# One-core decoder step on Trainium2: the compression of a unit runs with the next channel tile's products, and the first loads are cut and ordered anew

## The chip, the core and the metric

The kernel runs on one NeuronCore of a Trainium2 chip. That core has five engines that take their instructions in program order and meet at semaphores: TensorE (PE in the profile; its weight loads stand apart as PEld), VectorE (DVE), ScalarE (ACT), GpSimd (POOL) and SyncE (SP). SP and ACT also issue DMAs; sixteen DMA engines carry them. The metric is the device time of one execution in microseconds (us). It was 1530.45 us, the median of three runs from 1529.3 to 1533.97 us.

## What is computed

One inference step of two layers, all in float32, for a prompt of 512 tokens and 8 samples of 8 tokens (576 tokens in all), width 1024. The first layer is a gated depthwise convolution over 2048 channels; the second is attention with a compressed, a selected and a windowed branch. The change touches two pieces of it that share no data: the input product and convolution of the first layer, and the compression of the 8 samples' cached keys and values, which depends on inputs alone.

```python
def conv_mixer(x, state, w_in, b_in, dw_w, dw_b, ln_g, ln_b, w_out):
    h = x @ w_in + b_in
    a, gl, z = jnp.split(h, 3, axis=-1)
    u = a * jax.nn.sigmoid(gl)
    ...
    y = layer_norm(depthwise_31_taps(up), ln_g, ln_b)
    y = jax.nn.silu(y) * jax.nn.silu(z)
    return y @ w_out, new_state

def compress(kseq, pe, w1, b1, w2):
    ...
    h = jnp.einsum("sd,sdh->h", pe, w1) + b1
    for j in range(r):
        h = h + parts[j][:, j:j + nc]        # parts: 16-token chunks times w1
    return jnp.einsum("bcgh,hd->bcgd", jax.nn.silu(h), w2)
```

## The kernel before

**Tiles and units.** The 2048 channels are 16 tiles of 128. For each channel tile `ct`, PE makes two products of the transposed input `xT` (1024 x 576) with 512 KB of weights each: the gate (`product(2 * ct, GL, ...)`, called GL below) and the value (`product(2 * ct + 1, A, ...)`, called A). A product is 16 matmuls in the program, which the trace counts as 32. ACT takes the sigmoid of GL into the one buffer `sgl`, DVE multiplies (L996 to L1000) and then runs the 31 taps (L1014, some 29 us per tile), and POOL does the sample rows and sums. After all channel tiles come 16 Z products on the same line (L1354), and between the second and third of them four matmuls that sum `y` over the channels (L1450, L1451).

The compression is 16 **units** `u` (8 samples, keys and values). A unit's 2 MB of cache pages come into `xc`. It goes in four steps `k`: ACT copies a quarter into `rl` (`regroup`, L721), PE transposes it (`turn`, L1365), ACT copies the result to `xtr` (`turned_out`, L713), and PE multiplies it with `wc` (`hidden`, L1377). ACT then applies silu (L776), and PE multiplies with the second weight (`latent`, L1401 or L1406). In the kernel before, unit `ct` is worked in the loop turn of channel tile `ct`: GL, the transposes of the conv state (`state_turn`, L1387 to L1392), `turn(ct, 0)`, A, `latent(ct - 1)`, then the other three turns and four hiddens. In loop turn 0 the first `turn` stands behind A.

**Order.** Everything is written out by hand, engine by engine. SP issues, in order: x, the sample rows, the page table; then per channel tile the GL weights (L431), the state rows (L436), the A weights (L431), and 16 page loads of 128 KB for the unit (L444), each behind a register load of the page's number. ACT issues the conv parameters (L690 to L693: 37 rows of 2048 floats, one row to one partition of `aux`), small tensors, `wc` (L697) and the second weights (L700, L701) before its first copy. PE starts with the transposes of x (L384; 8 for each of four 128-token tiles and for the 64 sample tokens), waiting for both x loads together (`s_x`), then transposes `aux` (L1342, 16 of 37 x 128) and two small tensors (L1344); after the copies to `pars` (L705, L980) the first GL product may begin. POOL forms the bias sums `cbs` from `wc` (L600 to L604), and PE adds them up at the end of unit 0 (L1433).

**Buffers.** `wi` has 4 slots of weights, `xc` has 3 units (`XBUF`), the page loads of unit u wait until ACT has regrouped unit u - 3 (`rl_ready`). `bank[MISC]` in PSUM is shared in turn by state, latent and bias results; the order of turns is in `state_group` and `latent_group`.

Of the kernel before, what the change touches and what calls it, by code (L numbers as in the profile page):

```python
# [11 lines left out]
P = 128  # L12
# [30 lines left out]
NPAR = TAPS + 6  # L43
UPS = TS + TAPS - 1
# [40 lines left out]
def build_program(nc, x_prompt, x_sample, state_conv, cache_kv, cache_win, page_table,  # L85
# [4 lines left out]
    with ctx:  # L90
# [63 lines left out]
        aux = at(182, DIN)  # L154
        aux2 = at(190, P)
        cbt = at(140, 16 * P).rearrange("p (n h) -> p n h", n=16)
        cbs = at(192, 2 * P).rearrange("p (s h) -> p s h", s=2)
# [60 lines left out]

        def state_group(ct):

            return 1 if ct == 0 else 2 * ct + 1

        def latent_group(u):

            return 2 * u + 4
# [8 lines left out]
        s_small = sem("s_small")  # L234
        s_x = sem("s_x")
# [45 lines left out]
        ring_in = [sem(f"ring_in{r}") for r in range(8)]  # L281
# [142 lines left out]
        def _(sp):  # L424
            sp.dma_start(xr[:, 0:4, :], x_prompt[0].rearrange("(t p) m -> p t m", p=P)).then_inc(s_x, 16)
# [21 lines left out]

            for ct in range(CT):
                if ct >= 2:
                    sp.wait_ge(gl_ps, ct - 1)  # L450
                load_weights(2 * ct, 1, ct)
                if ct >= 2:
                    sp.wait_ge(misc_ps, state_group(ct - 2))
                load_state(ct)
                if ct >= 2:
                    sp.wait_ge(a_ps, ct - 1)
                load_weights(2 * ct + 1, 0, ct)
                if ct == 0:
                    sp.wait_ge(s_pg, 16)
# [38 lines left out]
            def load_group(n):  # L498
                for k in range(KT):
                    if n < 2:  # L500

                        sp.wait_ge(t4_used, 4 * n + k // 2 + 1)
                    elif k == 0:
                        sp.wait_ge(grp_used, n - 1)
                    sp.dma_start(ring[:, n % 2, k], w_in[k * P:(k + 1) * P, GROUPS[n]:GROUPS[n] + 512]
                                 ).then_inc(ring_in[(n % 2) * 4 + k // 2], 16)
# [182 lines left out]
        def _(act):  # L689
            act.dma_start(aux[0:TAPS, :], conv_dw_w[0]).then_inc(s_small, 16)  # L690
            act.dma_start(aux[TAPS:TAPS + 3, :], conv_b_in[0].rearrange("(a n) -> a n", a=3)).then_inc(s_small, 16)
            for r, v in enumerate((conv_dw_b, conv_ln_g, conv_ln_b)):
                act.dma_start(aux[TAPS + 3 + r:TAPS + 4 + r, :], v).then_inc(s_small, 16)  # L693
            act.dma_start(aux2[0:32, :], cmp_pe[0].rearrange("s (q e) d -> (s q) (e d)", e=2)).then_inc(s_small, 16)
            act.dma_start(aux2[32:34, :], cmp_b1[0]).then_inc(s_small, 16)
            for s in range(2):
                act.dma_start(wc[:, s].rearrange("p j q h -> p (j q) h"),  # L697
                              cmp_w1[0, s].rearrange("(q e) d h -> (e d) q h", e=2)).then_inc(s_wc, 16)
# [6 lines left out]
            act.copy(pars[:, 0:8].rearrange("p c n -> p (c n)"), bank[4][:, 0:8 * NPAR]).then_inc(s_aev, 1)  # L705
# [44 lines left out]

            for ct in range(CT):
# [8 lines left out]
                if ct == 0:  # L760
                    regroup(0, 0)
                turned_out(ct, 0)
                regroup(ct, 1)
                if ct:
                    latent_out(ct - 1)
                for k in range(1, STEPS):
                    turned_out(ct, k)
                    if k + 1 < STEPS:
                        regroup(ct, k + 1)
                if ct == 0:  # L770
                    act.wait_ge(misc_ps, 2)
                    act.activation(cb[:, 0:1], bank[MISC][:, 0:1], ACT.Identity, bias=auxT[:, 32:33])
                    act.activation(cb[:, 1:2], bank[MISC][:, 1:2], ACT.Identity, bias=auxT[:, 33:34]).then_inc(misc_ev, 1)
                    act.wait_ge(misc_ev, 2)
                act.wait_ge(xt_used, STEPS * (ct + 1))
                act.activation(hT[:, ct % 2, 0:4 * NC].rearrange("p (g n) -> p g n", g=4),  # L776
                               bank[HID][:, :].rearrange("p (g n) -> p g n", g=4)[:, :, 0:NC],
                               ACT.Silu, bias=cb[:, ct % 2:ct % 2 + 1]).then_inc(h_silu, 1)
                if ct + 1 < UNIT:
                    regroup(ct + 1, 0)  # L780
            state_rows(CT)
            latent_out(UNIT - 1)
# [10 lines left out]
            for i in range(2):  # L793
                silu_z(i)
# [180 lines left out]
        def _(dve):  # L975
# [4 lines left out]
            ch.mark(dve.tensor_copy(pars[:, 8:16].rearrange("p c n -> p (c n)"), bank[5][:, 0:8 * NPAR]))  # L980
# [55 lines left out]
            dve.wait_ge(s_x, 64)  # L1036
# [298 lines left out]
        def _(pe):  # L1335
            pe.wait_ge(s_const, 3)
            pe.wait_ge(s_x, 32)
            for t in range(TT):
                transpose_tile(pe, x_columns, t, PAIRS, s_xps, s_xev)
            pe.wait_ge(s_small, 112)  # L1340
            for c in range(CT):
                pe.transpose(bank[4 + c // 8][:, (c % 8) * NPAR:(c % 8 + 1) * NPAR], aux[0:NPAR, c * P:(c + 1) * P],  # L1342
                             ident[0:NPAR, 0:NPAR])
# [65 lines left out]

            for ct in range(CT):  # L1410
# [8 lines left out]
                if ct == 0:  # L1419
                    turn(0, 0)  # L1420
                    pe.wait_ge(s_wc, 32)
                    pe.wait_ge(s_w2, 48)
                else:
                    latent(ct - 1)
                for k in range(1, STEPS):
                    turn(ct, k)
                    hidden(ct, k - 1)
                hidden(ct, STEPS - 1)
                if ct == 0:
                    pe.wait_ge(s_cbs, 2)  # L1430
                    pe.wait_ge(misc_ev, 1)
                    for s in range(2):
                        last = pe.matmul(bank[MISC][:, s:s + 1], cbs[:, s], ones[:, 0:1], start=True, stop=True)  # L1433
                    last.then_inc(misc_ps, 1)
            state_turn(CT)
            latent(UNIT - 1)

            for i in range(CT):
# [4 lines left out]
                product(2 * CT + i, Z[i % 2], z_ps)  # L1443
                if i == 1:
# [36 lines left out]
            def kv_tile(w, t):  # L1481
# [36 lines left out]
            def wide(j):  # L1518
# [8 lines left out]
                for h in range(2):  # L1527
                    for k in range(KT):
                        if r == 0 and h == 0:
                            pe.wait_ge(ring_in[(n % 2) * 4 + k // 2], 32 * (n // 2 + 1))  # L1530
# [351 lines left out]
```

## Time and profile before

| | us |
|---|---|
| median of 3 runs | 1530.45 |
| the profiled execution | 1531.58 |
| its span, first to last instruction | 1529.9 |
| PE busy | 1434.4 (94%) |
| DVE busy | 818.3 (53%) |
| ACT busy | 476.0 (31%) |
| POOL busy | 480.1 (31%) |

The span is the stretch between the first and the last profiled instruction; 1.7 us of the execution lie outside it. A share of busy time is a mean over stages with different limits, so the stretch around a change is read by itself: the first 60 us, one loop turn, and the end of the loop near 600 us.

### The profile page before, as it was taken

Reading aid. Unit: us, or ns where it says so; the run is one execution under the profiler, and the core shown is the slowest. Engines: PE = TensorE matmul, PEld = TensorE weight load, DVE = VectorE, ACT = ScalarE, POOL = GpSimd, SP = SyncE. Lnnn points to the kernel's source line nnn. Section 1 sums busy time; section 2 is a strip of 40 time slices with the busy share of each in tenths; the row PEclk is TensorE's granted clock in tenths of the full one; section 3 lists DMA queues with packets and bytes.
Section 4 is the critical chain, followed back from the end, with each engine's and each line's share of the span. In section 5 each row is a group of like instructions: output and inputs, shape, how many; then the busy total and the mean of one; then the engine's idle time right before and its main releaser. Section 6 shows DMA issues by size and latency. Waiting matters only on the chain.

```text
span 1529.9 us, 23043 instructions
## 1 busy us (share of the span) xinstructions
PE 1434.4 (94%) x8098; PEld 910.8 (60%) x8098; DVE 818.3 (53%) x1663; ACT 476.0 (31%) x1063; POOL 480.1 (31%) x449
## 2 busy tenths in 40 slices
PE   2999999999999999999999999999988889988886
PEld 2666666666666666777444444877755554455543
DVE  1578887888888888710112311132367774454443
ACT  1243343334434333222100000111355552064552
POOL 0855556566665555411100000000056562000000
PEclk9999999999999999999999999999999999999998
DMA  6543332333333312533510333114000004537870
GB/s 183 137 122 115 91 106 87 93 104 97 95 98 98 96 32 67 190 110 96 228 68 0 115 114 123 50 58 163 28 1 1 2 1 133 184 111 243 256 236 9
DMA packets 139549, 158.38 MB, mean 104 GB/s; under 512 B 16226, under 2 KB 103525, under 8 KB 139237
## 3 DMA queue, kind: packets, MB, share of 16 engines
q1 hardware_dynamic: 134162, 150.07, 31.5%
q10 hardware_dynamic: 5272, 6.83, 1.5%
q8 instruction: 65, 1.06, 0.3%
q14 instruction: 50, 0.41, 0.1%
HBM read 150.18 MB, written 16.38 MB: 109 GB/s over the span
## 4 chain that ended last, share of the span: by engine, by line
PE 84%; SPq 4%; DVE 3%; POOL 3%; issue 2%; ACTq 2%; DMA 2%; ACT 1%; DVEq 0%
PE bank L1354 25%; PE bank L1377 15%; PE bank L1531 8%; PE bank L1466 7%; PE bank L1493 5%; PE bank L1365 4%; PE bank L1693 4%; POOL arena L679 3%; PE bank L1639 2%; SPq L546 2%; PE bank L1670 2%; SPq L548 2%; PE bank L1654 2%; DMA arena<-in_cache_kv_dram 2%; DVE arena L1154 2%
## 5 line engine op out<-in xcount | busy, mean ns | idle before, releaser
L1014 DVE SCALAR_TENSOR_TENSOR arena<-arena 128x512 f32<-128x512 f32 x464 | 424.3, 988 | 0.0
L1354 PE MATMUL bank<-arena 128*128 128x288 f32 x1536 | 381.0, 408 | 0.9 <-DVE arena L981 0.9
L1354 PEld LDWEIGHTS bank<-arena 128*128 128x128 f32 x1536 | 292.0, 191 | 86.5 <-issue 8.3
L1377 PE MATMUL bank<-arena 128*128 128x508 f32 x512 | 239.8, 615 | 0.0
L1377 PEld LDWEIGHTS bank<-arena 128*128 128x128 f32 x512 | 93.3, 190 | 109.8 <-issue 109.8
L613 POOL TENSOR_TENSOR arena<-arena 128x248 f32<-128x248 f32 x128 | 134.1, 1082 | 1.3
L1531 PE MATMUL bank<-arena 128*128 128x288 f32 x512 | 127.0, 407 | 0.6 <-PE bank L1531 0.6
L398 DVE SCALAR_TENSOR_TENSOR arena<-arena,bank 128x512 f32<-128x512 f32 (+1 forms) x20 | 13.6, 680 | 209.8 <-PE bank L1466 160.8
L679 POOL TENSOR_SCALAR arena<-arena 128x128 f32<-128x128 f32 (+3 forms) x96 | 100.3, 1055 | 71.8 <-DVE arena L1162 71.8
L1531 PEld LDWEIGHTS bank<-arena 128*128 128x128 f32 x512 | 96.2, 190 | 27.3 <-issue 1.5
L1466 PE MATMUL bank<-arena 128*128 128x512 f32 x256 | 110.4, 592 | 0.0
L713 ACT COPY arena<-bank 128x512 f32<-128x512 f32 x128 | 68.7, 589 | 108.7 <-PE bank L1365 91.4
L620 POOL TENSOR_TENSOR arena<-arena 128x1024 f32<-128x1024 f32 (+1 forms) x64 | 97.0, 1516 | 5.0
L1154 DVE CUSTOM_DVE_ANT_0 arena<-bank,arena 128x512 f32<-128x512 f32 (+3 forms) x128 | 57.6, 489 | 53.2 <-PE bank L1639 52.8
L1466 PEld LDWEIGHTS bank<-arena 128*128 128x128 f32 x256 | 48.5, 190 | 59.9 <-issue 59.6
L1493 PE MATMUL bank<-arena 128*128 128x512 f32 x192 | 83.3, 593 | 0.6 <-PE bank L1496 0.6
L625 POOL TENSOR_TENSOR arena<-arena 128x576 f32<-128x576 f32 x16 | 18.4, 1147 | 181.7 <-DVE arena L1016 181.7
L1654 PE MATMUL bank<-arena 128*128 128x128 f32 x320 | 54.9, 291 | 20.3 <-POOL arena L679 19.3
L721 ACT COPY arena<-arena 128x512 f32<-128x512 f32 x128 | 73.2, 627 | 0.2 <-DMA arena<-in_cache_kv_dram 0.2
L1365 PEld LDWEIGHTS bank<-arena 128*128 128x128 f32 x512 | 59.1, 141 | 22.1 <-issue 21.1
L886 ACT ACTIVATE arena<-arena 128x512 f32<-128x512 f32 (+3 forms) x128 | 70.8, 556 | 1.5 <-DVE arena L1154 0.8
L1365 PE MATMUL bank<-arena 128*128 128x128 f32 x512 | 66.6, 273 | 2.4 <-ACT arena L721 2.4
(254 smaller groups left out, 1585.7 us busy)
## 6 DMA issues: line engine op xcount, KB each, us to landing
arena<-in_cache_kv_dram SPq DMA_DIRECT2D x256, 128.0 KB, 3.4
arena<-in_cache_kv_dram SPq DMA_DIRECT2D x128, 256.0 KB, 3.2
arena<-in_conv_w_in_dram SPq DMA_DIRECT2D x48, 512.0 KB, 4.2
arena<-in_nsa_w_in_dram SPq DMA_DIRECT2D x56, 256.0 KB, 4.7
arena<-in_conv_w_out_dram SPq DMA_DIRECT2D x16, 512.0 KB, 4.8
arena<-in_cache_win_dram SPq DMA_DIRECT2D x8, 1024.0 KB, 7.1
out_dram<-in_cache_win_dram SPq DMA_DIRECT2D x1, 8064.0 KB
arena<-in_x_prompt_dram SPq DMA_DIRECT2D x2, 2048.0 KB, 9.4
```

The costliest lines, as they stand in the source:

```text
L613: ch.mark(pool.tensor_tensor(terms[:, :, n, 0:TAPS], ups[c][:, :, n:n + TAPS], pars[:, ct:ct + 1, 0:TAPS].broadcast_to([P, NB, TAPS]), ALU ...
L620: ch.link(pool.tensor_tensor(flat[:, :, 0:half], flat[:, :, 0:half], flat[:, :, half:2 * half], ALU.add))
L679: pool.tensor_scalar(w, w, ust[:, 36 + k:37 + k], None, ALU.mult).then_inc(u_sc, 1)
L1014: ch.mark(dve.scalar_tensor_tensor(part, src, w, part, ALU.mult, ALU.add))
L1154: dve.tensor_tensor_reduce(prob[u % SLOTS][:, e, 0:n], bank[2 * (u % 2) + e][:, 0:n], maskrow[:, 512 - n:512], 1.0, BIG, ALU.add, ALU.min, ...
L1354: last = pe.matmul(bank[pair + h][:, 0:HALF], wi[:, n % WSLOT, k], xT[:, k, h * HALF:(h + 1) * HALF], start=k == 0, stop=k == KT - 1)
L1365: last = pe.transpose(bank[TURN + g // 2][:, col:col + P], rlf[:, g, h], ident)
L1377: last = pe.matmul(out, wc[:, s, j, h * STEPS + k], x4[:, h, :, j:j + NC], start=(k == 0 and h == 0 and j == 0), stop=(k == STEPS - 1 and ...
L1466: last = pe.matmul(bank[pair + nh][:, :], y[:, c, t * P:(t + 1) * P], wo[c][:, nh * 512:(nh + 1) * 512], start=c == 0, stop=c == CT - 1)
L1493: last = pe.matmul(bank[t][:, :], x1T[:, k, t * P:(t + 1) * P], slot, start=k == 0, stop=k == KT - 1)
L1531: last = pe.matmul(bank[pair + h][:, 0:HALF], ring[:, n % 2, k, r * P:(r + 1) * P], x1T[:, k, h * HALF:(h + 1) * HALF], start=k == 0, stop ...
L1654: last = pe.transpose(bank[4 + e][:, k * P:(k + 1) * P], prob[u % SLOTS][:, e, k * P:(k + 1) * P], ident)
```

## The change

Five things are changed.

1. The parameters are loaded as 16 partitions (one for each channel tile) of 31, 3 or 1 pieces of 128 floats, instead of as rows of 2048 floats to 31, 3 or 1 partitions. PE then needs 37 transposes of 16 x 128 in place of 16 of 37 x 128, and the copies to `pars` write with a stride.
2. x is loaded in four DMAs of 512 KB with a semaphore each, and PE waits tile by tile.
3. `wc` is issued by SP instead of ACT, behind the first A weights; the weights and state rows of channel tiles 0 and 1 are issued ahead of the first unit's pages.
4. Unit `u` is worked in loop turn `u + 1`; its first `turn` stands ahead of that loop turn's A product. Unit 15 stands behind the loop, and `latent(15)` behind the first Z product.
5. Later, in the second layer, eight semaphores of the weight ring become four, so the first matmul of a group waits for four pieces instead of two.

```diff
-            sp.dma_start(xr[:, 0:4, :], x_prompt[0].rearrange("(t p) m -> p t m", p=P)).then_inc(s_x, 16)
+            for t in range(4):
+                sp.dma_start(xr[:, t, :], x_prompt[0, t * P:(t + 1) * P, :]).then_inc(x_in[t], 16)
...
+            for ct in range(2):
+                load_weights(2 * ct, 1, ct)
+                load_state(ct)
+                load_weights(2 * ct + 1, 0, ct)
+                if ct == 0:
+                    for s in range(2):
+                        sp.dma_start(wc[:, s].rearrange("p j q h -> p (j q) h"),
+                                     cmp_w1[0, s].rearrange("(q e) d h -> (e d) q h", e=2)).then_inc(s_wc, 16)
+            sp.wait_ge(s_pg, 16)
             for ct in range(CT):
                 if ct >= 2:
                     sp.wait_ge(gl_ps, ct - 1)
-                load_weights(2 * ct, 1, ct)
-                if ct >= 2:
+                    load_weights(2 * ct, 1, ct)
...
                 if ct == 2:
-                    sp.wait_ge(misc_ps, 2)
+                    sp.wait_ge(s_aps, 1)
...
-            act.dma_start(aux[0:TAPS, :], conv_dw_w[0]).then_inc(s_small, 16)
+            act.dma_start(aux[0:CT, 0:TAPS], conv_dw_w[0].rearrange("k (c n) -> c k n", c=CT)).then_inc(s_small, 16)
...
+            def unit(u):
+                turned_out(u, 0)
+                regroup(u, 1)
+                if u:
+                    latent_out(u - 1)
...
                 state_rows(ct)
-                if ct == 0:
+                if ct:
+                    unit(ct - 1)
+                else:
                     regroup(0, 0)
...
             state_rows(CT)
-            latent_out(UNIT - 1)
+            unit(UNIT - 1)
...
             pe.wait_ge(s_const, 3)
-            pe.wait_ge(s_x, 32)
             for t in range(TT):
+                pe.wait_ge(x_in[t] if t < 4 else s_x, 16)
                 transpose_tile(pe, x_columns, t, PAIRS, s_xps, s_xev)
             pe.wait_ge(s_small, 112)
-            for c in range(CT):
-                pe.transpose(bank[4 + c // 8][:, (c % 8) * NPAR:(c % 8 + 1) * NPAR], aux[0:NPAR, c * P:(c + 1) * P],
-                             ident[0:NPAR, 0:NPAR])
+            for k in range(NPAR):
+                half, col = divmod(k, PHALF) if k < 2 * PHALF else (1, PHALF)
+                pe.transpose(bank[4 + half][:, col * CT:(col + 1) * CT], aux[0:CT, k], ident[0:CT, 0:CT])
...
                 product(2 * ct, GL, gl_ps)
                 state_turn(ct)
                 if ct:
-                    turn(ct, 0)
+                    turn(ct - 1, 0)
                     pe.wait_ge(a_free, ct)
                 product(2 * ct + 1, A, a_ps)
...
+                if ct:
+                    unit(ct - 1)
             state_turn(CT)
-            latent(UNIT - 1)
+            turn(UNIT - 1, 0)
+            unit(UNIT - 1)
...
                 product(2 * CT + i, Z[i % 2], z_ps)
+                if i == 0:
+                    latent(UNIT - 1)
...
                     if t == 0:
-                        pe.wait_ge(ring_in[(w % 2) * 4 + k // 2], 32 * (w // 2 + 1))
+                        pe.wait_ge(ring_in[(w % 2) * 2 + k // 4], 64 * (w // 2 + 1))
```

**SP at the start of the program.** Before, the rows up to the first page load (128x8x128 is a tile of weights, 120x2x128 the state rows):

```order
L425 DMA arena<-in_x_prompt_dram 128x4x1024
L426 DMA arena<-in_x_sample_dram 64x1024
L427 DMA pages<-in_page_table_dram 1x128
L431 DMA arena<-in_conv_w_in_dram 128x8x128
L436 DMA arena<-in_state_conv_dram 120x2x128
L431 DMA arena<-in_conv_w_in_dram 128x8x128
L443 TENSOR_LOAD pages
```

And now, where line 441 loads weights, 446 state rows and 464 `wc`:

```order
L435 DMA arena<-in_x_prompt_dram 128x1024 x4
L436 DMA arena<-in_x_sample_dram 64x1024
L437 DMA pages<-in_page_table_dram 1x128
L441 DMA arena<-in_conv_w_in_dram 128x8x128
L446 DMA arena<-in_state_conv_dram 120x2x128
L441 DMA arena<-in_conv_w_in_dram 128x8x128
L464 DMA arena<-in_cmp_w_dram 128x16x128 x2
L441 DMA arena<-in_conv_w_in_dram 128x8x128
L446 DMA arena<-in_state_conv_dram 120x2x128
L441 DMA arena<-in_conv_w_in_dram 128x8x128
L453 TENSOR_LOAD pages
```

Five more DMAs stand ahead of the first page load: the two of `wc`, and those of channel tile 1, which stood behind the first unit's 16 pages.

**PE at the start of the program.** Before, from the transposes of x through GL 0 and A 0 (L1354) into unit 0:

```order
L384 MATMUL bank<-arena 128x128 x32
L384 MATMUL bank<-arena 128x64 x8
L1342 MATMUL bank<-arena 128x37 x16
L1344 MATMUL bank<-arena 128x34
L1354 MATMUL bank<-arena 128x288 x16
L1387 MATMUL bank<-arena 128x120 x2
L1354 MATMUL bank<-arena 128x288 x16
L1365 MATMUL bank<-arena 128x128 x16
L1377 MATMUL bank<-arena 128x4x127 x4
L1365 MATMUL bank<-arena 128x128 x8
```

And now (L1373 is the product, L1384 `turn`, L1406 to L1411 the state):

```order
L393 MATMUL bank<-arena 128x128 x32
L393 MATMUL bank<-arena 128x64 x8
L1362 MATMUL bank<-arena 128x16 x37
L1363 MATMUL bank<-arena 128x34
L1373 MATMUL bank<-arena 128x288 x16
L1406 MATMUL bank<-arena 128x120 x2
L1373 MATMUL bank<-arena 128x288 x32
L1406 MATMUL bank<-arena 128x120 x2
L1410 MATMUL bank<-arena 30x128
L1411 MATMUL bank<-arena 64x128
L1384 MATMUL bank<-arena 128x128 x8
L1373 MATMUL bank<-arena 128x288 x16
```

A 0 and GL 1 now follow each other, and the first `turn` of unit 0 stands between GL 1 and A 1.

**PE at the end of the loop.** Before, from the last hiddens of unit 15 to the first sum over channels:

```order
L1377 MATMUL bank<-arena 128x4x127 x8
L1391 MATMUL bank<-arena 30x128
L1392 MATMUL bank<-arena 64x128
L1401 MATMUL bank<-arena 127x64 x4
L1354 MATMUL bank<-arena 128x288 x32
L1450 MATMUL bank<-arena 128x288
```

And now, from the last state transposes to `latent(15)` (L1425 is `latent(14)`, L1396 a hidden, L1420 `latent(15)`):

```order
L1410 MATMUL bank<-arena 30x128
L1411 MATMUL bank<-arena 64x128
L1384 MATMUL bank<-arena 128x128 x8
L1425 MATMUL bank<-arena 128x254 x2
L1384 MATMUL bank<-arena 128x128 x8
L1396 MATMUL bank<-arena 128x4x127 x4
L1384 MATMUL bank<-arena 128x128 x8
L1396 MATMUL bank<-arena 128x4x127 x4
L1384 MATMUL bank<-arena 128x128 x8
L1396 MATMUL bank<-arena 128x4x127 x8
L1373 MATMUL bank<-arena 128x288 x16
L1420 MATMUL bank<-arena 127x64 x4
```

Unit 15 now stands between the loop and Z 0 with no product of 128x288 inside it.

## Rows read from the trace of the kernel before

**Rows 1.** PE's waits from 60 to 760 us: waiting, releaser, us, times, longest.

```profile
PE bank L1401 <- ACT arena L735: 0.9, 1, 0.9
```

**Rows 2.** Timeline, first 60 us: start, us, engine, line, operands, count, idle before.

```profile
2.89 17.67 SPq L436 DMA_DIRECT2D arena<-in_state_conv_dram  x1
...
5.28 18.36 ACTq L697 DMA_DIRECT2D arena<-in_cmp_w_dram  x1
...
23.84 4.50 PE L384 MATMUL bank<-arena 128*128 128x128 f32 x20 [23.84 <-DMA arena<-in_x_sample_dram]
25.15 23.05 SPq L444 DMA_DIRECT2D arena<-in_cache_kv_dram  x16
...
31.02 3.87 PE L384 MATMUL bank<-arena 128*128 128x128 f32 x20 [2.68 <-ACT arena L373]
...
34.68 1.86 PE L1342 MATMUL bank<-arena 37*128 37x37 f32 x16
...
37.51 10.77 PE L1354 MATMUL bank<-arena 128*128 128x288 f32 x32 [0.86 <-DVE arena L981]
...
50.92 20.89 SPq L444 DMA_DIRECT2D arena<-in_cache_kv_dram  x16
...
56.10 1.04 PE L1365 MATMUL bank<-arena 128*128 128x128 f32 x8
```

**Rows 3.** DMA issues of the first 26 us: count, KB each, us to landing.

```profile
arena<-in_x_sample_dram SPq DMA_DIRECT2D x1, 256.0 KB, 22.4
arena<-in_conv_dw_w_dram ACTq DMA_DIRECT2D x1, 248.0 KB
```

**Rows 4.** Windows: us, busy of PE, PEld, DVE, ACT, POOL, granted clock, DMA share, GB/s.

```profile
3.00:8.00 5.00, 0.00 (x0) 0.00 (x0) 0.00 (x0) 0.65 (x2) 0.00 (x0) 1.00 1.01 382
10.00:15.00 5.00, 0.00 (x0) 0.00 (x0) 0.00 (x0) 0.00 (x0) 0.00 (x0) 1.00 1.07 264
16.00:21.00 5.00, 0.00 (x0) 0.00 (x0) 0.00 (x0) 0.00 (x0) 0.00 (x0) 1.00 0.09 35
...
60.20:63.60 3.40, 3.40 (x8) 1.79 (x7) 3.40 (x4) 2.11 (x4) 3.40 (x4) 0.50 0.34 100
113.40:148.10 34.70, 34.70 (x142) 22.78 (x141) 29.08 (x36) 13.48 (x25) 20.14 (x19) 1.00 0.40 116
```

**Rows 5.** Time to landing, first of the page loads L444, then of the weights L431.

```profile
DMA to landing us min/median/max: 3.2/4.1/6.3
...
DMA to landing us min/median/max: 3.7/4.2/8.0
```

**Rows 6.** Timeline of PE: unit 0, then loop turn 1 and the start of turn 2.

```profile
59.53 1.33 PE L1365 MATMUL bank<-arena 128*128 128x128 f32 x8 [2.40 <-ACT arena L721]
...
78.21 0.50 PE L1433 MATMUL bank<-arena 128*128 128x1 f32 x4
78.57 8.01 PE L1354 MATMUL bank<-arena 128*128 128x288 f32 x32
...
87.71 7.93 PE L1354 MATMUL bank<-arena 128*128 128x288 f32 x32
95.47 1.02 PE L1406 MATMUL bank<-arena 128*128 128x254 f32 x4
96.33 1.03 PE L1365 MATMUL bank<-arena 128*128 128x128 f32 x8
...
113.36 7.92 PE L1354 MATMUL bank<-arena 128*128 128x288 f32 x32
```

**Rows 7.** Timeline: ACT behind a unit and around its state rows, and PE's first sum.

```profile
114.14 1.13 ACT L721 COPY arena<-arena 128x512 f32<-128x512 f32 x2
...
573.48 0.25 ACT L734 COPY arena<-bank 30x128 f32<-30x128 f32 x1
...
575.00 1.07 ACT L713 COPY arena<-bank 128x512 f32<-128x512 f32 x2 [1.11 <-issue]
...
617.01 0.65 PE L1450 MATMUL bank<-arena 128*128 128x288 f32 x2
```

More of the change, by code:

```diff
@@ L43 @@
 NPAR = TAPS + 6
+PHALF = NPAR // 2
 UPS = TS + TAPS - 1
@@ L217, in build_program @@
         gate_rows = nc.dram_tensor("gate_rows", (NB * TS, 48), F32, kind="Internal").ap()
+        misc_turns = [("state", 0), ("state", 1), ("bias", 0)]
+        for n in range(2, CT + 1):
+            misc_turns += [("state", n), ("latent", n - 2)]
+        misc_turns.append(("latent", UNIT - 1))
         def state_group(ct):
-            return 1 if ct == 0 else 2 * ct + 1
+            return misc_turns.index(("state", ct)) + 1
         def latent_group(u):
-            return 2 * u + 4
+            return misc_turns.index(("latent", u)) + 1
+        bias_group = misc_turns.index(("bias", 0)) + 1
         def weights_in(n):
@@ L234, in build_program @@
         s_small = sem("s_small")
+        x_in = [sem(f"x_in{t}") for t in range(4)]
         s_x = sem("s_x")
@@ L280, in build_program @@
         x1_ev = [sem(f"x1_ev{w}") for w in range(2)]
-        ring_in = [sem(f"ring_in{r}") for r in range(8)]
+        ring_in = [sem(f"ring_in{r}") for r in range(4)]
         wg_in = sem("wg_in")
@@ L749, in latent_out @@
                     act.copy(kcT[:, b].rearrange("p g n -> p (g n)"), bank[MISC][:, 0:2 * NC]).then_inc(misc_ev, 1)
+            def unit(u):
[3 more added lines that the diff above has]
+                    latent_out(u - 1)
+                for k in range(1, STEPS):
+                    turned_out(u, k)
+                    if k + 1 < STEPS:
+                        regroup(u, k + 1)
+                if u == 0:
+                    act.wait_ge(misc_ps, bias_group)
+                    act.activation(cb[:, 0:1], bank[MISC][:, 0:1], ACT.Identity, bias=auxT[:, 32:33])
+                    act.activation(cb[:, 1:2], bank[MISC][:, 1:2], ACT.Identity, bias=auxT[:, 33:34]).then_inc(misc_ev, 1)
+                    act.wait_ge(misc_ev, bias_group)
+                act.wait_ge(xt_used, STEPS * (u + 1))
+                act.activation(hT[:, u % 2, 0:4 * NC].rearrange("p (g n) -> p g n", g=4),
+                               bank[HID][:, :].rearrange("p (g n) -> p g n", g=4)[:, :, 0:NC],
+                               ACT.Silu, bias=cb[:, u % 2:u % 2 + 1]).then_inc(h_silu, 1)
+                if u + 1 < UNIT:
+                    regroup(u + 1, 0)
             for ct in range(CT):
@@ L791, in silu_z @@
                 last.then_inc(z_free, 1)
-            for i in range(2):
-                silu_z(i)
+            silu_z(0)
+            latent_out(UNIT - 1)
+            silu_z(1)
             act.wait_ge(var_ready, 1)
@@ L1408, in latent, with unit @@
                 last.then_inc(misc_ps, 1)
+            def unit(u):
+                if u:
+                    latent(u - 1)
+                else:
+                    pe.wait_ge(s_wc, 32)
+                    pe.wait_ge(s_w2, 48)
+                for k in range(1, STEPS):
+                    turn(u, k)
+                    hidden(u, k - 1)
+                hidden(u, STEPS - 1)
+                if u == 0:
+                    pe.wait_ge(s_cbs, 2)
+                    pe.wait_ge(misc_ev, bias_group - 1)
+                    for s in range(2):
+                        last = pe.matmul(bank[MISC][:, s:s + 1], cbs[:, s], ones[:, 0:1], start=True, stop=True)
+                    last.then_inc(misc_ps, 1)
             for ct in range(CT):
```

67 lines of the change are left out of this document (14 added, 53 removed).

## The prediction

> **What bounds the kernel now.** I read the table of busy shares first: PE is busy 94% of the span. Then PE's own waits: from 60 to 760 us there is one, of 0.9 us [rows 1]. So in the loop over channel tiles, and well past it, time is what PE executes. A reordering gains nothing there unless it takes PE instructions away, and this one doesn't. The room is in front of it. The timeline shows PE idle until 23.84 us, released by the landing of x_sample; its first product starts at 37.51 [rows 2].
>
> Why does 256 KB need 22.4 us to land [rows 3]? The windows say it. From 3 to 8 us the DMA engines are all busy at 382 GB/s, from 10 to 15 us at 264 GB/s, and from 16 to 21 us the busy share is 0.09 at 35 GB/s [rows 4]. A share of 0.06 is one engine of sixteen. So 15 engines have run dry and about one still works through a list, and everything issued that has a piece behind it waits: x_sample, and SP and ACT, whose next issues take 17.67 and 18.36 us [rows 2]. What differs from the other loads is the 37 parameter rows, the 248 KB of conv_dw_w above all [rows 3]: at one engine's pace, between 35 GB/s (row of 16 to 21 us, all traffic) and 382/16 = 24 GB/s, the 37 rows (some 0.30 MB) are 9 to 13 us of one engine, and its share of x is interleaved with them. That is about the tail seen.
>
> The Trainium skill says so outright (DMA: Bandwidth & Descriptors, "Why a DMA increments its semaphore by 16 and not by 1"): a DMA uses the largest number of engines up to 16 that divides the slowest dimension on both sides; 31, 3 and 1 rows give one engine, 16 partitions give 16. The windows agree, and by that rule the tail goes wholly.
>
> **The start of products, T0.** New parameter loads: the same 0.30 MB on 16 engines. x and the sample rows are 2.36 MB; at 382 GB/s from about 2 us on they are over near 9 us, the first tile near 3.5. I put its landing at 5. PE then has 40 transposes of x, 4.50 + 3.87 = 8.4 us [rows 2], at 13.4 us. Parameters: 16 transposes took 1.86, 0.116 each [rows 2]; I take 37 x 0.116 = 4.3 us. No row has 16 x 128: if the time went with rows it would be 37 x 0.05 = 1.9, and at the 0.225 of a 128-row transpose (4.50/20) 8.3. From L1342's end to the product, with the small transpose and the copies, 37.51 - 34.68 - 1.86 = 1.0. T0 = 5 + 8.4 + 4.3 + 1.0 = 18.7, between 16 and 23. The strided copies to pars have no row of their own; they lie inside that 1.0, and double that is covered by the same bounds. ACT is free of wc's 18.36 us of issue and no longer holds up the x copies (2.68 us before).
>
> **But T0 doesn't decide; the pages do.** The first turn of unit 0 now stands ahead of A 1. GL 0 and A 0 take 56.10 - 37.51 = 18.6 us, GL 1 with the state transposes 87.71 - 78.57 - 1.04 = 8.1 [rows 2, 6]. PE wants the turn at T0 + 26.7 = 45.4. It needs all 16 pages of unit 0, and five DMAs were put ahead of them. In front of the pages, both queues together: x 2.36 MB, then parameters 0.32, four weight tiles 2.10, wc 2.10 (its 128 partitions x 16 KB), states 0.25, second weights 0.10, that is 4.87 MB. At 382 GB/s for x and 264 for the rest: 1.9 + 6.2 + 18.4 = 26.5 us. SP runs ahead of the transfers by what the queue takes. Before, it stalled at L436 with x, samples and one weight tile posted [rows 2], per engine 32 + 4 + 64 pieces; a hundred 512-byte pieces on each of 16 engines are 0.8 MB, 3 us. If the limit goes by time instead, it was 8 us. I take S = 24 for the first page issue (from 18.5 to 26.5). That is hardly earlier than the 25.15 of before.
> 16 issues take 20.89 us (23.05 in the first unit, against the tail) [rows 2], landing 3.2 [rows 5]: 48.1. Regroup 1.13 [rows 7]: 49.3. So PE waits some 4 us at that turn. Then turn 1.04, A 1 95.47 - 87.71 = 7.8, the rest of unit 0 113.36 - 96.33 = 17.0, its bias sums 78.57 - 78.21 = 0.4 [rows 6]: GL 2 at 75.5. Before, a wait of 2.40 us was followed by a stretch of granted clock 0.50, the lower level of 1.2 GHz [rows 4, 6], and unit 0 took 78.21 - 59.53 = 18.7 instead of 17.0. I expect the same 1.65 behind the new wait: GL 2 at 77.1, where it was at 113.36.
>
> **What is owed later.** Before GL 2 the old order had done units 0 and 1, the new one only unit 0. Unit 15 comes behind the loop: turn 1.04, latent 0.86, rest 17.0, together 18.9. In the loop each turn hides behind a product; here none does. Silu and regroup end 114.14 + 1.13 - 113.36 = 1.9 us after the last hidden [rows 6, 7]; PE has 0.3 us of state transposes meanwhile: 1.6 idle. Then ACT does its state rows and their two DMA issues (575.00 - 573.48 = 1.5 [rows 7]), turned_out 1.07 and regroup 1.13: 1.9 + 1.5 + 2.2 = 5.6, where PE, with turn and latent done, is free at 3.9: 1.7 idle. Together 3.3. The 0.9 wait of L1401 goes, since latent(15) is behind Z 0.
> The first sum (L1450) was at 617.0. Now 617.0 - 36.3 + 18.9 - 0.9 + 3.3 = 602.0, 15.0 us earlier.
>
> **At no cost.** In the loop DVE is busy 29.1 us of a turn of 34.7 us and POOL 20.1 [rows 4]. A 1 comes 16 us behind A 0, so DVE takes it late, at about 38 + 29 = 67, ahead of the state transposes of turn 2, at 85; without that cover PE would wait us for us. POOL's bias sums start when wc lands, near 22, and are due at 75; a whole turn's work of POOL fits in twice. The ring semaphores of the second layer add two more pieces to the wait of a group's first matmul; the groups are loaded one ahead, so I take nothing, and 1 us at most without the cover. Everything behind the first sum keeps its order.
>
> So the profiled execution of 1531.6 becomes 1516.6; the median shown lies 1.1 lower: **1515.5**.
>
> **Rivals.**
> *The queue runs further ahead or the first loads are faster* (S = 18.5): the pages land at 42.6, the turn waits for nothing, GL 2 is at 45.4 + 26.2 = 71.6: 5.5 us more, 1510. For it: ACT's and SP's stalls before were of a jammed engine, not of a full queue. Against: bytes are bytes, and 16 issues have cost 20.9 in every unit.
> *The crowd is worse*: S = 26.5, 23 us of issue as in the first unit, half clock behind the gaps of unit 15 too (1.65): 2.5 + 2.1 + 1.65 = 6 worse, 1521.5.
> *The parameters still run on one engine*, in 592 pieces: x_sample again at 24, T0 at 39 with the longer transposes; the turn is then hidden, GL 2 at 39 + 26.7 + 26.2 = 92, first sum 616.9: 1530.4, no change. Against: the pieces are spread over 16 partitions as those of wc and the weights are, and those fill all engines.
> *Slower: the weights of GL 2 queue behind 32 page loads.* SP is in order; they are issued after two units of pages, at S + 41.8, landing up to 8.0 later [rows 5]: 73.8, due at 75.5 to 77. Before, they were issued at 71.8 too but due at 113. Each us beyond costs one. It would turn the sum at 15 us more, if 32 issues took 60 us (1.9 each instead of 1.3): at 2.1 each, GL 2 at 24 + 67 + 8 = 99, 1537. Against: the longest 16 took 23.05.
>
> The Trainium skill has a rule against the cut (DMA: Bandwidth & Descriptors, "Measured (HBM→SBUF, 128 partitions, SWDGE, issued from GpSimd)"): at least 1 MiB per DMA for three quarters of peak; x now goes in 512 KB, the parameters in less. By its fixed 2 us per DMA, not overlapped, an estimate is 8 us more for x. The trace doesn't bear it out: weight tiles of 512 KB land in 4.2 us at the median beside other traffic.
>
> **Numbers.** The forecast 0.55, further ahead 0.22, crowd 0.12, one engine 0.05, weights late 0.03, and 0.03 for a harm I don't see. A measurement tells 0.3%, 4.6 us, from no change. The range from 1508 to 1522 holds the first three. Faster 0.91, same 0.05, slower 0.04.
>
> **What would show it.** No stretch near one engine's share in the first 25 us; x_sample landing near 10; first product at 16 to 23; page loads starting at 24; a PE wait of 2 to 5 us for L734 at the first turn, then half clock; GL 2 at 72 to 79; loop turns of 34.7 as before; two PE gaps of 1.6 and 1.7 behind the loop; the first sum near 602. I am wrong if the loop turns get longer, if pages start well before 20, or if PE waits for weights at GL 2.

## The result, and the profile after

The changed kernel runs in 1518.7 us at the median of 6 runs (1516.1 to 1520.7), the one before, on the same chip, in 1529.9 (6 runs, 1526.8 to 1534.4): ratio 0.9919 [0.9901, 0.9938], 11 to 12 us faster. The profiled execution takes 1517.71 us (span 1516.0) beside 1531.58 of before. The forecast was 1515.5 us, 15.0 us earlier, in a range from 1508 to 1522.

The start first, as in [rows 2, 3]. The timeline of PE in the first 52 us of the changed kernel (start, us, line, operands, count, idle before and its releaser):

```profile
5.55 1.94 PE L393 MATMUL bank<-arena 128*128 128x128 f32 x8 [5.55 <-DMA arena<-in_x_prompt_dram]
8.96 5.21 PE L393 MATMUL bank<-arena 128*128 128x128 f32 x32 [1.47 <-DMA arena<-in_x_prompt_dram]
14.11 2.47 PE L1362 MATMUL bank<-arena 16*128 16x16 f32 x37
17.75 9.69 PE L1373 MATMUL bank<-arena 128*128 128x288 f32 x32 [0.99 <-DVE arena L1000]
...
51.27 1.97 PE L1384 MATMUL bank<-arena 128*128 128x128 f32 x8 [7.68 <-ACT arena L734]
53.04 9.66 PE L1373 MATMUL bank<-arena 128*128 128x288 f32 x32
```

PE begins at 5.55 instead of 23.84 and the first product at 17.75 instead of 37.51, 19.8 us earlier. Part of it is given back: the first turn, whose pages had been there in time before, waits 7.68 us, and A 1 behind it takes 9.66 us for a product that costs 7.93 elsewhere. (The very first eight transposes take 1.94 us, as long as the eight of the turn at a granted clock of 0.50, 1.97, although the clock column below reads 1.00 for them. So the column can't be taken at its word for the first microseconds.)

The DMA side, SP's queue in time (an issue group's duration is what SP spent on it), then one row of the table of issues (count, KB, us to landing):

```profile
4.39 4.40 SPq L446 DMA_DIRECT2D arena<-in_state_conv_dram  x1
...
9.63 7.79 SPq L464 DMA_DIRECT2D arena<-in_cmp_w_dram  x2
...
25.49 43.86 SPq L454 DMA_DIRECT2D arena<-in_cache_kv_dram  x32
```

```profile
arena<-in_x_sample_dram SPq DMA_DIRECT2D x1, 256.0 KB, 10.7
```

And windows as in [rows 4] (from:to, length, busy of PE, PEld, DVE, ACT, POOL, granted clock, DMA share, GB/s):

```profile
3.00:9.00 6.00, 1.98 (x9) 1.61 (x9) 0.69 (x1) 1.87 (x2) 0.00 (x0) 1.00 1.09 245
10.00:17.00 7.00, 6.63 (x67) 6.18 (x65) 2.71 (x5) 2.34 (x5) 1.09 (x2) 1.00 1.16 280
17.00:26.00 9.00, 8.25 (x27) 6.26 (x28) 0.61 (x4) 0.43 (x1) 0.00 (x0) 0.81 1.08 290
46.30:56.50 10.20, 5.22 (x16) 4.22 (x17) 10.20 (x10) 4.57 (x11) 10.12 (x9) 0.50 0.31 97
```

The stretch at share 0.09 is gone: the engines stay full through the first 26 us, and x_sample lands in 10.7 us instead of 22.4. But SP's first page issue is at 25.49, where it was at 25.15. Products start 20 us earlier, pages don't. The last window is the price: the granted clock is 0.50 (1.2 GHz) for 10.2 us around the wait.

ACT's regroup of unit 0, which waits for the last of the pages; the waits of PE from 60 to 760 us (the view of [rows 1]); and PE at the end of unit 0 and behind the loop:

```profile
50.08 1.14 ACT L734 COPY arena<-arena 128x512 f32<-128x512 f32 x2 [20.13 <-DMA arena<-in_cache_kv_dram]
```

```profile
PE bank L1384 <- ACT arena L734: 3.2, 2, 1.6
```

```profile
79.92 8.01 PE L1373 MATMUL bank<-arena 128*128 128x288 f32 x32
114.71 7.92 PE L1373 MATMUL bank<-arena 128*128 128x288 f32 x32
...
567.76 1.09 PE L1384 MATMUL bank<-arena 128*128 128x128 f32 x8 [1.58 <-ACT arena L734]
...
571.29 1.09 PE L1384 MATMUL bank<-arena 128*128 128x128 f32 x8 [1.57 <-ACT arena L734]
...
604.78 0.65 PE L1475 MATMUL bank<-arena 128*128 128x288 f32 x2
```

GL 2 starts at 79.92 (113.36 in [rows 6]), a loop turn is still 114.71 - 79.92 = 34.8 us, and the first sum is at 604.78 (617.01 in [rows 7]): 12.2 us earlier.

I compare kernels by this mark, the start of the first sum, below, beside the ratios. The last stage, the attention of the samples, takes 190.6 to 197.5 us in the profiled executions (from PE's first instruction on L1736 of the changed kernel to the end), and both of these ends are the changed kernel's own, in two executions. So an effect of 2 to 5 us at the start is read from marks of single profiles and only bounded by the totals.

The fifth part of the change, the ring's fewer semaphores, costs nothing that shows: from the first sum to the first score matmul of the prompt's attention (L1639, now L1664) it is 1103.81 - 617.01 = 486.80 us before and 1091.59 - 604.78 = 486.81 now.

### The profile page after: what moved, and what is told of

The parts are those of the page before. It is cut to its first block, busy times and chain, and to the rows that moved or that the text cites. A ratio compares the mean times of both kernels' runs of the same rounds, so it can differ in the third digit from the quotient of the medians.

```text
span 1516.0 us, 23089 instructions
## 1 busy us (share of the span) xinstructions
PE 1434.8 (95%) x8119; PEld 910.8 (60%) x8119; DVE 831.5 (55%) x1663; ACT 472.5 (31%) x1059; POOL 482.5 (32%) x449
## 3 DMA queue, kind: packets, MB, share of 16 engines
q8 instruction: 65, 1.06, 0.3%
## 4 chain that ended last, share of the span: by engine, by line
PE 83%; SPq 6%; DVE 3%; POOL 3%; issue 2%; DMA 2%; ACT 1%; ACTq 0%; DVEq 0%
PE bank L1373 23%; PE bank L1396 15%; PE bank L1556 8%; PE bank L1491 7%; PE bank L1518 5%; PE bank L1384 4%; PE bank L1718 4%; POOL arena L694 3%; PE bank L1664 2%; PE bank L1679 2%; PE bank L1695 2%; SPq L561 2%; SPq L563 2%; DMA arena<-in_cache_kv_dram 2%; DVE arena L1173 2%
## 5 line engine op out<-in xcount | busy, mean ns | idle before, releaser
L1033 DVE SCALAR_TENSOR_TENSOR arena<-arena 128x512 f32<-128x512 f32 x464 | 429.5, 999 | 0.0
L1373 PE MATMUL bank<-arena 128*128 128x288 f32 x1536 | 381.7, 409 | 1.0 <-DVE arena L1000 1.0
L1373 PEld LDWEIGHTS bank<-arena 128*128 128x128 f32 x1536 | 292.6, 191 | 86.9 <-issue 8.5
L1396 PE MATMUL bank<-arena 128*128 128x508 f32 x512 | 238.4, 612 | 0.0
L1396 PEld LDWEIGHTS bank<-arena 128*128 128x128 f32 x512 | 92.6, 188 | 108.9 <-issue 108.9
L1384 PEld LDWEIGHTS bank<-arena 128*128 128x128 f32 x512 | 59.5, 142 | 31.2 <-issue 18.5
L1384 PE MATMUL bank<-arena 128*128 128x128 f32 x512 | 67.3, 275 | 10.8 <-ACT arena L734 10.8
L640 POOL TENSOR_TENSOR arena<-arena 128x576 f32<-128x576 f32 x16 | 18.3, 1146 | 175.1 <-DVE arena L1035 175.1
```

The costliest lines, as they stand in the source:

```text
L1033: ch.mark(dve.scalar_tensor_tensor(part, src, w, part, ALU.mult, ALU.add))
L1373: last = pe.matmul(bank[pair + h][:, 0:HALF], wi[:, n % WSLOT, k], xT[:, k, h * HALF:(h + 1) * HALF], start=k == 0, stop=k == KT - 1)
L1384: last = pe.transpose(bank[TURN + g // 2][:, col:col + P], rlf[:, g, h], ident)
L1396: last = pe.matmul(out, wc[:, s, j, h * STEPS + k], x4[:, h, :, j:j + NC], start=(k == 0 and h == 0 and j == 0), stop=(k == STEPS - 1 and ...
```

## The experiments

The ratios compare each kernel with the kernel before on the same chip. The theory after the result: the gain is set by when unit 0's pages are in place, and the wait for them costs more than its own length, since the clock halves behind it. The rivals: T0, the start of the first product, sets it; the loads ahead of the pages don't matter; the half clock comes with something else.

**Each half alone.** The kernel before with only the parameters laid out on 16 partitions:

```diff
-act.dma_start(aux[0:TAPS, :], conv_dw_w[0]).then_inc(s_small, 16)
+act.dma_start(aux[0:CT, 0:TAPS], conv_dw_w[0].rearrange("k (c n) -> c k n", c=CT)).then_inc(s_small, 16)
```

> The kernel before with one edit: the parameters on 16 partitions (37 transposes of 16 rows). Theory (one DMA engine held everything up): the stretch near one engine's share from 16 to 21 us is gone, x_sample lands near 15 us instead of 23.8, the first product starts between 22 and 28 us instead of 37.5, the wait of 2.4 us inside unit 0 stays; the total is 10 to 15 us under before, 1515 to 1520, as much as the whole change. Rival (the gain is that of the moved compression or of the tiles of x): under 3 us.

1522.0 us (10 runs, 1516.6 to 1525.6), ratio 0.9936 [0.9913, 0.9959]. First product at 30.55, first sum at 607.32, 9.7 us earlier. That is less than expected: the total is 2 us above the 1515 to 1520, and the first product more than 2 us late. ACT's own issues of wc and w2 stood ahead of its copies of x (`ACTq` was held 6.65 us at wc and 5.86 at w2), which before were hidden in the tail. PE and SP:

```profile
21.39 3.87 PE L385 MATMUL bank<-arena 128*128 128x128 f32 x20 [4.07 <-ACT arena L374]
...
30.55 9.65 PE L1357 MATMUL bank<-arena 128*128 128x288 f32 x32 [0.99 <-DVE arena L984]
...
51.45 1.06 PE L1368 MATMUL bank<-arena 128*128 128x128 f32 x8 [2.40 <-ACT arena L723]
```

```profile
14.51 23.92 SPq L445 DMA_DIRECT2D arena<-in_cache_kv_dram  x16
```

With wc on ACT's queue and channel tile 1's loads behind the pages, SP reaches the pages at 14.51, 11 us before the changed kernel does. The wait of 2.40 us inside unit 0 stays as expected, but here no half clock follows it: the turn behind it takes 1.06 us and the unit from this turn on 17.1, where before, behind the same 2.40, it took 18.7.

The kernel before with only the units shifted by one channel tile (loop body):

```diff
 if ct:
-    turn(ct, 0)
+    turn(ct - 1, 0)
...
-    turn(0, 0)
...
+if ct:
+    unit(ct - 1)
 state_turn(CT)
+turn(UNIT - 1, 0)
+unit(UNIT - 1)
```

> The kernel before with one edit: unit u is worked in loop turn u + 1. Theory: the first product stays at 37.5; the wait of 2.4 us and its half clock (1.65) in unit 0 go, two gaps of 1.6 us come behind the loop; the total is 0 to 4 us under before, 1526 to 1530, which five rounds may not tell from none. Rival (the moved compression brings the gain): 8 us or more.

1527.5 us (12 runs, 1524.5 to 1538.3), ratio 0.9992 [0.9971, 1.0014]: no difference that the runs tell. First product 36.21, GL 2 87.74, first sum 612.60, 4.4 us earlier. Of these 1.3 are the start, where the second half of x's transposes took 2.58 us instead of 3.87; no edit of this run touches them. The two gaps of 1.6 us behind the loop are there as in the changed kernel.

**The changed kernel with the parameters as rows again** (the first diff backwards):

> The changed kernel with the parameters again as 31, 3 and 1 rows, all else as changed. Theory: one DMA engine is late again; the tiles of x land by 17 to 19 us, the first product is at 24 to 28, but the pages of unit 0 land at 55 to 60 instead of 50.1, so the turn ahead of A 1 waits longer: 5 to 10 us over the changed kernel, 1523 to 1529. Rival (the order of loads and the tiles carry the gain): within 2 us of the changed kernel's 1518.7.

1526.9 us (12 runs, 1524.9 to 1532.2), ratio 0.998 [0.9962, 0.9998]. First sum 612.76. The jam is back, in SP's issue of the states, and with it a late first product (27.83) and late pages (first issue at 33.78), all as expected; the turn waits 4.30 us, and GL 2 is at 87.89, 8.0 behind the changed kernel's:

```profile
4.32 15.21 SPq L446 DMA_DIRECT2D arena<-in_state_conv_dram  x1
...
33.78 43.65 SPq L454 DMA_DIRECT2D arena<-in_cache_kv_dram  x32
```

```profile
59.23 1.97 PE L1382 MATMUL bank<-arena 128*128 128x128 f32 x8 [4.30 <-ACT arena L733]
60.99 9.66 PE L1371 MATMUL bank<-arena 128*128 128x288 f32 x32
```

So the layout of 0.3 MB carries most of the gain: without it, all the rest of the change gets 4.2 of the 12.2 us. The same bytes cost SP 4.40 us of stall with 16 partitions, 15.21 with rows. The Trainium skill's rule (DMA: Bandwidth & Descriptors, "Why a DMA increments its semaphore by 16 and not by 1"), by which a slowest dimension of 31 gives one engine and one of 16 gives sixteen, agrees with that. At the first sum the parameters alone get 9.7 and all the rest 4.2, 13.9 in sum, and together they get 12.2.

**wc behind unit 0's pages:**

```diff
-                if ct == 0:
-                    for s in range(2):
-                        sp.dma_start(wc[:, s]...).then_inc(s_wc, 16)
...
                 load_unit(ct)
+                if ct == 0:
+                    for s in range(2):
+                        sp.dma_start(wc[:, s]...).then_inc(s_wc, 16)
```

> The changed kernel with the 2 MB of wc issued by SP behind the pages of unit 0 instead of ahead of them. Theory (the pages bound the first loop turns): the first page issue moves from 25.5 to about 17.5, the pages land near 42 instead of 50.1, the wait of 7.7 us at the first turn and the half clock after it go, GL 2 starts near 70 instead of 79.9: 8 to 10 us under the changed kernel, 1508 to 1511. Rival (the start is bound by something else, or wc is then late for unit 0): the gap moves to the first hidden of unit 0 and the total stays within 3 us of 1518.7.

1520.7 us (7 runs, 1517.8 to 1522.2), ratio 0.9936 [0.9912, 0.996]. First sum 605.60. Half of the theory held: pages are issued from 17.21, and the turn at 43.68 waits for nothing. But the rival won the other half: the wait moved, to the end of the unit, and the total stayed within the rival's 3 us of 1518.7:

```profile
43.68 1.04 PE L1384 MATMUL bank<-arena 128*128 128x128 f32 x8
44.55 7.93 PE L1373 MATMUL bank<-arena 128*128 128x288 f32 x32
...
76.95 1.01 PE L1443 MATMUL bank<-arena 128*128 128x1 f32 x4 [7.43 <-POOL arena L619]
77.83 10.90 PE L1373 MATMUL bank<-arena 128*128 128x288 f32 x32
```

Again 7 us of wait, again a product behind it too long (10.90 for 8.01, the clock at 0.50 in 73.4 to 83.7). A late wc alone would not have cost it, by this sum: POOL starts on it at 49.88, and the bias sums took 18.3 us of POOL in the changed kernel, so they would be there at 68.2, before PE asks at 69.5. They took 27.0 us. DVE is at its taps by then, and POOL's first operation alone takes three times as long, 7 us more (first this kernel, then the changed one, where DVE was idle):

```profile
49.88 10.62 POOL L615 TENSOR_TENSOR arena<-arena 128x2048 f32<-128x2048 f32 x1 [34.30 <-DMA arena<-in_cmp_w_dram]
```

```profile
26.18 3.61 POOL L615 TENSOR_TENSOR arena<-arena 128x2048 f32<-128x2048 f32 x1 [10.85 <-DMA arena<-in_cmp_w_dram]
```

**The changed kernel once more**, unedited, beside these on their chip:

> The changed kernel itself, beside the next three on one chip: 1516 to 1520, 10 to 13 us under before, with the wait near 7.7 us at the first turn.

1520.8 us (6 runs, 1519.2 to 1525.1), ratio 0.9933 [0.9914, 0.9951]. The first product is at 18.50, the first page issue at 24.37 and the regroup at 50.05. The wait is 6.34, shorter than the expected 7.7 because PE comes later; the clock is 0.50 from 46.9 to 57.1, GL 2 at 80.22, the first sum at 605.09, 0.3 from the first profile. This mark repeats to a few tenths, the first page issue only to 1.1 us.

**Half of unit 0's pages issued by ACT:**

```diff
-for n in range(NPG):
+for n in range(NPG if u else NPG // 2):
...
+act.wait_ge(s_pg, 16)
+for n in range(NPG // 2, NPG):
+    pg = act.value_load(pages[0:1, n:n + 1], ...)
+    act.dma_start(xc[(n % 8) * 16:(n % 8) * 16 + 16, 0, n // 8], ...).then_inc(xc_in[0], 16)
```

> The changed kernel with 8 of unit 0's 16 pages issued by ACT, right behind its copy of the parameters; wc stays ahead, so POOL's bias sums are not late. Theory (the first loop turns wait for the issue of 16 pages at 1.3 us each on one queue): the pages land near 40 us, no wait at the first turn, no half clock on A 1, GL 2 near 70 instead of 79.9, 8 to 10 us under the changed kernel. Rival (the transfers, not the issues, bound the landing, or ACT's issues hold up the sigmoid of GL 0): pages land at 46 or later, under 4 us gained.

1512.0 us (6 runs, 1507.7 to 1517.6), ratio 0.9884 [0.9859, 0.9908]. What stands ahead of SP's pages is the same (25.28); ACT issues its eight from 19.23 in 10.53 us, so they also start 6 us ahead of SP's, not behind the loads of channel tile 1. The regroup starts at 43.27 instead of 50.05. No wait, full clock, GL 2 at 71.59 and the first sum at 596.47, 8.6 us before the changed kernel's:

```profile
45.56 1.04 PE L1390 MATMUL bank<-arena 128*128 128x128 f32 x8
46.44 7.93 PE L1379 MATMUL bank<-arena 128*128 128x288 f32 x32
...
71.59 8.01 PE L1379 MATMUL bank<-arena 128*128 128x288 f32 x32
```

The pages came some 3 us later than the expectation had them, in time all the same. One queue that issues 16 loads, each behind a page number read into a register, at 1.3 to 1.4 us apiece, had been the limit: in the changed kernel the DMA share is down to 0.27 from 35 to 40 us, and a page lands 3.5 us behind its issue (median). Here the share is 1.14 in the same stretch, SP's eighth is out at 37.7, and pages take 6.3 us (SP's) and 9.9 us (ACT's) at the median: now the transfers are the limit. The regroup is 6.8 us earlier; how much of this is ACT's earlier start and how much the second queue, no run separates.

**x in one DMA again**, all else as changed:

```diff
-for t in range(4):
-    sp.dma_start(xr[:, t, :], x_prompt[0, t * P:(t + 1) * P, :]).then_inc(x_in[t], 16)
+sp.dma_start(xr[:, 0:4, :], x_prompt[0].rearrange("(t p) m -> p t m", p=P)).then_inc(s_x, 16)
```

> The changed kernel with x again in one DMA and PE waiting for both x loads. Theory (the pages decide, not the first product): PE starts near 13.5 instead of 5.5, the first product at 21 to 24 instead of 17.7, the wait at the first turn is shorter by the same 4 to 6 us, and the total is within 1.5 us of the changed kernel. Rival (the tiles of x bring part of the gain): 4 us or more over it.

1516.7 us (5 runs, 1514.6 to 1520.2), ratio 0.9911 [0.9888, 0.9933]. Both expectations missed. The totals don't tell it from the changed kernel; the mark does: first sum at 601.13, 4 us earlier than with tiles on the same chip. PE in time, and the window in which the changed kernel had its 0.50:

```profile
13.02 6.83 PE L393 MATMUL bank<-arena 128*128 128x128 f32 x40 [13.02 <-DMA arena<-in_x_sample_dram]
...
23.88 10.24 PE L1372 MATMUL bank<-arena 128*128 128x288 f32 x32 [0.99 <-DVE arena L999]
...
50.18 1.09 PE L1383 MATMUL bank<-arena 128*128 128x128 f32 x8
51.11 7.93 PE L1372 MATMUL bank<-arena 128*128 128x288 f32 x32
```

```profile
46.30:56.50 10.20, 10.20 (x50) 8.09 (x49) 10.20 (x10) 4.58 (x11) 10.04 (x9) 1.00 0.32 99
```

The first product is 5.4 us later (23.88 for 18.50), so PE meets the turn at 50.18 when the pages have just landed. No wait, hence no half clock: the turn takes 1.09 instead of 1.97 and A 1 7.93 instead of 9.98. That is 2.9 of the 4 us; the other 1.1 is that the pages were in place 1.06 us sooner (regroup 48.99 for 50.05). Starting earlier bought nothing but a longer wait. It also bears on the rule of 1 MiB per DMA that the prediction weighed (the Trainium skill, DMA: Bandwidth & Descriptors, "Measured (HBM→SBUF, 128 partitions, SWDGE, issued from GpSimd)"). All of x and the sample rows were there at 13.0 us with x in one load, and with tiles the sample rows, last in line, landed at 2.75 + 10.7 = 13.4, so four loads of 512 KB cost some 0.4 us here.

**The first turn of unit 0 behind A 1**, which takes the wait off its place without moving a byte:

```diff
-                if ct:
+                if ct > 1:
                     turn(ct - 1, 0)
+                if ct:
                     pe.wait_ge(a_free, ct)
                 product(2 * ct + 1, A, a_ps)
+                if ct == 1:
+                    turn(0, 0)
```

> The changed kernel with unit 0's first turn behind A 1 instead of ahead of it (one turn moved on PE, no load and no other engine touched). Theory (the wait of 6 to 8 us for the pages and the half clock after it are what the first loop turns lose): A 1 runs at full clock while the pages land, unit 0 then has a wait of 2.4 us between its first two turns, GL 2 starts at 72 to 74 instead of 80, the first sum at 597 to 600 instead of 605, the total 5 to 8 us under the changed kernel. Rival (the loss lies in the transfers themselves, whatever PE does meanwhile): GL 2 at 78 or later.

1515.7 us (4 runs, 1513.4 to 1517.6), ratio 0.991 [0.9893, 0.9926], 3 to 5 us under the changed kernel's two medians, where 5 to 8 was expected.

```profile
43.91 7.93 PE L1373 MATMUL bank<-arena 128*128 128x288 f32 x32
51.67 1.04 PE L1384 MATMUL bank<-arena 128*128 128x128 f32 x8
56.10 1.94 PE L1384 MATMUL bank<-arena 128*128 128x128 f32 x8 [3.39 <-ACT arena L734]
57.84 4.26 PE L1396 MATMUL bank<-arena 128*128 128x508 f32 x8
...
74.85 8.01 PE L1373 MATMUL bank<-arena 128*128 128x288 f32 x32
```

A 1 now runs in the time of the wait and at full clock. Only the second regroup shows, 3.39 us that no product hides (1 us more than expected), with 3.3 us at a clock of 0.50 behind it. GL 2 is at 74.85, a little past the expected 72 to 74, and the first sum at 599.72, 5.4 us before the unedited kernel's. With the pages as late as ever, the wait and what followed it was that loss.

**Unit 15 between the Z products, on top of the pages by two:**

```diff
+z_product(0)
 turn(UNIT - 1, 0)
+z_product(1)
 unit(UNIT - 1)
+z_product(2)
+latent(UNIT - 1)
```

> The kernel of the previous run, and behind the loop Z 0 ahead of unit 15's first turn, Z 1 behind it, the sums over channels behind Z 2. Theory (the two gaps of 1.6 us are PE waiting for ACT with no product beside): both gaps go, 3 us under the previous run, more if a half clock behind them goes too. Rival (the work behind the sums becomes late): the same time or slower.

1509.2 us (4 runs, 1507.8 to 1512.5), ratio 0.9856 [0.9832, 0.988]: the fastest, some 21 us under the kernel before. All waits of PE from 40 to 760 us:

```profile
PE bank L1392 <- ACT arena L740: 0.8, 1, 0.8
PE bank L1485 <- ACT arena L766: 0.7, 1, 0.7
```

The first is unit 0's first turn, at 46.39, for pages that came 1.9 us later than in the run before. Behind the loop only the second is left, ahead of the sums, where there were two of 1.6. The sums stand one product later in this order, so their mark doesn't compare; the first product with `out` comes 632.7 us behind GL 2 instead of 635.5, 2.8 us sooner than in the pages-by-two kernel. The totals of those two overlap, so that it is faster than the pages alone rests on the mark.

## Why the prediction was near, and which term was off

The forecast of 1515.5 was 3.2 us too low and inside its range. The profiled execution (1517.71 for 1516.6) looks nearer than it should, by luck: it was 2.8 us behind the forecast at the first sum and 1.1 more up to the last stage, and then that stage, which varies by 7 us by itself, took 190.6 us instead of the 193.4 of before.

- *PE bounds the loop, only the front has room*: held. Loop turns 34.8 us, no wait of PE between 60 and 567 us.
- *One engine's tail makes x late, and 16 partitions end it*: shown both ways, by the parameters alone (9.7 us earlier) and by their return to rows (8 us of the 12 gone). That it is one engine is worked out from the share of 0.09; no view shows the engines singly. The prediction worked its rule out too widely: by the rule as it quotes it, 3 rows go to three engines. The 31 rows, 248 KB of the 0.30 MB, are the part that it puts on one.
- *T0 = 18.7*: 17.75 (18.50 in the second profile). Landing 5.55 for 5. The 37 parameter transposes took 2.47, predicted 4.3: the granted clock was 1.00 there; at 0.50, with the parameters alone, they took 4.13. The 8.4 for x was 7.15 plus 1.47 of waiting for a tile.
- *T0 doesn't decide*: right, and more so than I had it. Giving 5.4 us of T0 back made the mark 4 us earlier (1.1 of these because the pages came sooner).
- *S = 24 (S is the first page issue) and 16 issues in 20.9, turn at 49.3*: S 25.49 and 43.86 / 2 = 21.9 for 16 issues, turn at 51.27. In the second profile S was 24.37, as forecast, and 16 issues took 22.4; the regroup began at 50.05 all the same. So the pages' 2 us are the issues' pace as much as S. The limit by bytes was near: SP was held up at the states and in wc, as if the queue took about what I assumed.
- *The wait of 4 us, then 1.65 of half clock, GL 2 at 77.1*: **the mis-sized term.** PE was 1.8 us earlier than forecast and the pages 2.0 later: 7.68 us of wait. PE's part of that costs nothing, since the pages decide; the pages' part does. The half clock covered the turn too (1.97 for 1.04) and A 1 (9.66 for 7.93), 2.7 us instead of 1.65. The 1.65 was taken from a wait of 2.40 us; with the rows put back, a wait of 4.30, near the 4 of the forecast, also cost 2.7. GL 2 was at 79.92, 2.8 late, which is the whole miss at the first sum: 604.78 for 602.0. The experiments with the turn moved, x whole and pages by two each took this wait away and got 4 to 8.6 us.
- *18.9 and 3.3 owed behind the loop, 0.9 gone*: gaps of 1.58 and 1.57 for 1.6 and 1.7. From GL 2 to the first sum the forecast's sum gives 524.9, measured 604.78 - 79.92 = 524.9.
- *The rivals.* Further ahead: no, S was 24 to 25.5, not 18.5. Weights late at GL 2: no; they were issued at 69.39, where the sum had 24 + 41.8 = 65.8, and GL 2 began at 79.92 without a wait for them. The crowd: S came more than half way to its 26.5 in one profile and not in the other, 16 page issues took 21.9 and 22.4, not 23, and no half clock followed unit 15's gaps (the turns there take 1.09).
- *The parameters still on one engine*: no; x_sample landed in 10.7 us. *The 1 MiB rule*: its estimate of 8 us was that of four loads at 2 us each; against one load it would be 6, and some 0.4 showed.
- *Costs at nothing*: in the changed kernel POOL's sums and DVE's late A 1 held up nobody, and the ring's semaphores cost nothing (486.8 us on either side). That POOL was covered only as long as wc came early, the kernel with wc behind the pages showed.

Not settled: what sets S. It was 24.07 to 25.49 in four kernels and five profiles that have the same loads in the same order on SP ahead of the pages, and no run changed the number of loads without their bytes.

## What to carry to other kernels

A load that lands late for its size may be held up by a small neighbour that runs on one or two DMA engines: look for a stretch where the DMA share drops to that of one engine while issues are stalled. When the start is sped up, find the next thing that must be in place and move it by as much, or put other work of the bound engine ahead of it; a wait gives back its length and then, with TensorE's clock, it can give back more. Loads whose addresses are read into registers are costly to issue one by one (1.3 to 1.4 us apiece here, where SP issued a weight tile in some 0.4 to 0.6 when nothing held it up): two engines issuing them gained 8.6 us at the mark, more than any reordering that was tried.

## What the runs showed of the hardware that was not expected

DVE and POOL slow each other. POOL's 128x2048 fp32 multiplication, the first step of the bias sums, takes 3.61 us with DVE idle and 10.62 beside 12 of DVE's taps and the addition that follows them. DVE's taps ran on at 0.6 us each meanwhile, and then the addition (L1035) took 3.99 us where it takes 0.69 in the changed kernel: first POOL lost, then DVE. The other way round, the 29 taps take 19.29 us in the kernel with wc behind the pages, where POOL is idle for the first 12 us and then in that one operation, and 26.57 in the kernel before, where POOL is at short operations for 16 us of them:

```profile
37.73 19.29 DVE L1033 SCALAR_TENSOR_TENSOR arena<-arena 128x512 f32<-128x512 f32 x29
```

```profile
583.48 26.57 DVE L1014 SCALAR_TENSOR_TENSOR arena<-arena 128x512 f32<-128x512 f32 x29
```

In the kernel with wc behind the pages POOL's second multiplication of this kind took 3.94 us, and DVE spent at least 2.5 us in a single tap (0.67 on average in the first of these rows), as the window of that time shows in its third group, x1:

```profile
68.00:70.50 2.50, 1.52 (x4) 0.38 (x2) 2.50 (x1) 0.00 (x0) 2.50 (x1) 1.00 1.14 275
```

The slow clock isn't confined to the wait, and what it costs isn't in proportion to the wait. What a wait of PE cost on the work behind it, beyond its own length:

| kernel | wait, us | stretch at a granted clock of 0.50, us | cost behind the wait, us |
|---|---|---|---|
| changed | 7.68 | 10.2 | 2.7 |
| wc behind the pages | 7.43 | 10.3 | 3.4 |
| changed, second profile | 6.34 | 10.2 | 3.0 |
| rows again | 4.30 | 6.8 | 2.7 |
| first turn behind A 1 | 3.39 | 3.3 | 1.4 |
| before | 2.40 | 3.4 | 1.65 |
| parameters only | 2.40 | none | none |
| changed, behind the loop | 1.58, 1.57 | none | none |

The four waits of 4.3 to 7.7 us cost 2.7 to 3.4 each, in no order of their length; the shorter ones cost about half of that or nothing, and the same 2.40 us did both. Why, no run shows.
